# Third layer's attention: outputs scaled in place of probabilities, and TensorE visits it every second slot

## The reference, cut to what matters

```python
proj = y @ w_in; q, k, v = split(proj)                     # stage in3
s = einsum('bqhgd,bjhd->bhgqj', q_c, k_c) * scale + bias
p = softmax(where(valid, s, -inf))                         # p / sum(p)
o = einsum('bhgqj,bjhd->bqhgd', p, v_c)
return o.reshape(B, S, C_DIM) @ w_out                      # stage out3
```

## Time and profile before

| | us |
|---|---|
| runs | 2072.51, 2074.53, 2071.71 (median 2072.51) |
| profiled execution | 2075.14 |
| its span | 2073.3 |
| TensorE busy in it | 2055.2 |
| VectorE busy | 1180.8 |
| ScalarE busy | 759.5 |

### The profile page before, as it was taken

The page is one execution under the profiler, slowest core; times in us unless marked ns, Lnnn a source line. Parts: engine busy times, 40 slices in busy tenths (PEclk is TensorE's granted clock), DMA queues, the critical chain, the costliest instruction groups (busy, mean ns, idle before and its releaser), DMA issues.

```text
span 2073.3 us, 27109 instructions
## 1 busy us (share of the span) xinstructions
PE 2055.2 (99%) x10366; PEld 1689.7 (81%) x10366; DVE 1180.8 (57%) x1927; ACT 759.5 (37%) x1163; POOL 123.8 (6%) x138
## 2 busy tenths in 40 slices
PE   9999999999999999999999999999999999999999
PEld 7888888778888888988788888888876688888887
DVE  5444433786444433487778666633668877666433
ACT  5222222354322222463454322222557753222222
POOL 0000000400000000000002000000413120000001
PEclk9999999999999999999999999999999999999999
DMA  8322233312222222331221322233347622232222
GB/s 255 121 98 101 76 99 108 130 47 96 86 101 101 96 69 98 116 102 62 92 82 62 101 101 101 76 99 109 103 128 166 158 78 102 101 101 95 72 96 82
DMA packets 78300, 210.90 MB, mean 102 GB/s; under 512 B 46192, under 2 KB 49568, under 8 KB 61840
## 3 DMA queue, kind: packets, MB, share of 16 engines
q1 hardware_dynamic: 72896, 184.04, 28.0%
q0 software_dynamic: 2992, 12.31, 2.1%
q10 hardware_dynamic: 2336, 13.52, 1.8%
HBM read 195.08 MB, written 7.38 MB: 98 GB/s over the span
## 4 chain that ended last, share of the span: by engine, by line
PE 88%; DVE 6%; ACT 3%; issue 1%; DMA 1%; POOL 0%; SPq 0%; ACTq 0%; DVEq 0%
PE ps L1184 28%; PE ps L1185 28%; PE ps L1186 28%; ACT weigh L561 2%; DVE w_lo L1629 1%; PE ps L684 1%; DVE weigh L576 1%; DVE halves L583 1%; PE ps L666 1%; ACT w_hi L1621 1%; PE ps L651 1%; DVE weigh L593 1%; DMA h<-in_x_t 0%; ACT x_split L1707 0%; PE ps L1171 0%
## 5 line engine op out<-in xcount | busy, mean ns | idle before, releaser
L1184 PE MATMUL ps<-x_split,w_hi 128*128 128x512 f32 (+1 forms) x1774 | 697.6, 393 | 1.2 <-DVE x_split L1667 1.2
L1186 PE MATMUL ps<-x_split,w_lo 128*128 128x512 f32 (+1 forms) x1774 | 688.3, 388 | 0.0
L1185 PE MATMUL ps<-x_split,w_hi 128*128 128x512 f32 (+1 forms) x1774 | 688.1, 388 | 0.0
L1611 ACT ACTIVATE w_hi<-raw 128x2048 fp32r<-128x2048 f32 (+3 forms) x144 | 242.2, 1682 | 495.2 <-PE ps L1186 492.3
L1184 PEld LDWEIGHTS ps<-x_split,w_hi 128*128 128x128 f32 x1774 | 333.3, 188 | 79.2 <-issue 12.5
L1639 DVE TENSOR_TENSOR w_lo<-raw,w_hi 128x2048 fp32r<-128x2048 f32 (+3 forms) x144 | 287.9, 1999 | 179.7 <-ACT w_hi L1611 179.2
L1186 PEld LDWEIGHTS ps<-x_split,w_lo 128*128 128x128 f32 x1774 | 333.2, 188 | 68.5
L1185 PEld LDWEIGHTS ps<-x_split,w_hi 128*128 128x128 f32 x1774 | 333.5, 188 | 66.5 <-issue 1.0
L1184 PE MATMUL ps<-act,w_hi 128*128 128x512 f32 (+1 forms) x1026 | 376.9, 367 | 3.4 <-DVE w_lo L1629 3.1
L1185 PE MATMUL ps<-act,w_hi 128*128 128x512 f32 (+1 forms) x1026 | 372.9, 363 | 0.0
L1186 PE MATMUL ps<-act,w_lo 128*128 128x512 f32 (+1 forms) x1026 | 372.7, 363 | 0.0
(11 more groups left out here) (248 smaller groups left out, 1760.3 us busy)
## 6 DMA issues: line engine op xcount, KB each, us to landing
raw<-in_w_up SPq DMA_DIRECT2D x87, 1024.0 KB, 4.9
raw<-in_w_down SPq DMA_DIRECT2D x29, 768.0 KB, 4.2
raw<-in_w_in SPq DMA_DIRECT2D x20, 1024.0 KB, 4.9
raw<-in_w_down SPq DMA_DIRECT2D x29, 640.0 KB, 3.8
raw<-in_w_out SPq DMA_DIRECT2D x8, 1024.0 KB, 4.9
raw<-in_w_in ACTq DMA_DIRECT2D x8, 1024.0 KB, 5.5
skew<-scratch POOLq DMA_DIRECT2D x1, 5120.0 KB, 32.4
biases<-skew POOLq DMA_DIRECT2D x16, 256.0 KB, 4.3
```

Of the source, the lines that this page charges most:

```text
L1184: pe.matmul(own, hi, rhs_hi, start=start, stop=False)
L1185: pe.matmul(own, hi, rhs_lo, start=False, stop=False)
L1186: return pe.matmul(own, lo, rhs_hi, start=False, stop=stop)
L1611: eng.activation(w_hi[:, w], raw[:, w], ACT.Copy).then_inc(hi_rounded, 1)
```

## The change

- `SLOTS`: the first 22 slots lie at steps 88, 93, 98, 104, ... 200 (before: 21 slots at 84, 89, 94, ... 190), the last seven at 203, 206, 210, 213, 217, 220, 224 (before: eight at 196, 200, ... 224).
- TensorE does nothing in odd slots. In even slot i it does the scores of units i and i+1 and then the value products of units i-5 and i-4.
- VectorE no longer scales probabilities. It copies the halves first, then writes the reciprocals of the sums to `OUT_INV`. Eight times SP stores the reciprocals of a chunk to DRAM (128 partitions x 8 values of 4 bytes, the order turned) and loads them back as two rows, each broadcast over 64 partitions.
- When a chunk's value products are done and its factors have landed, VectorE multiplies the bank by the factors into `mix_raw` (new, slot 3c+7, for odd c below 7 slot 3c+8); ScalarE takes the high part from there, and VectorE the low part one slot later (for c = 7 in slot 28 too).
- The clearing of `ssum`, whose place holds factors, moves from the start of out3 to the end of its first pass.
- In in1 and in2 the transposes of the values move from 14 to 12 steps before the end.

```diff
-SLOTS = {84 + 16 * i // 3 if i < 21 else 196 + 4 * (i - 21): i for i in range(29)}
+SLOTS = {88 + 16 * i // 3 if i < 22 else 203 + 7 * (i - 22) // 2: i for i in range(29)}
+        MIX_AT = {NPARTS * c + 7 + (c % 2 if c < KD - 1 else 0): c for c in range(KD)}
+        REST_AT = {i + int(c < KD - 1): c for i, c in MIX_AT.items()}
 def slot_pe(pe, i):
+            if i % 2:
+                return
+            for u in (i, i + 1):
+                if u < STEPS:
+                    scores_pe(pe, u)
+            for u in (i - 5, i - 4):
+                if 0 <= u < STEPS:
+                    values_of_unit_pe(pe, u)
 # values_of_unit_pe: the bank of chunk c is free when
-                if s == 0 and c >= 2: pe.wait_ge(w_mix, c - 1)
+                if s == 0 and c >= 2: pe.wait_ge(w_mixed, c - 1)
+        def factors_out_sp(sp, c):
+            sp.wait_ge(w_inverted, NPARTS * (c + 1))
+            if c >= 2:
+                sp.wait_ge(w_mixed, c - 1)
+            rows = factors[c % 2 * 2:c % 2 * 2 + 2, :].rearrange("h (n q) -> q h n", q=P)
+            sp.dma_start(rows, inverses_of(c), allow_slow_non_contiguous=True).then_inc(f_written, 16)
+        def factors_in_sp(sp, c):
+            sp.wait_ge(f_written, 16 * (c + 1))
+            for hh in range(2):
+                row = factors[c % 2 * 2 + hh:c % 2 * 2 + hh + 1, :]
+                sp.dma_start(factor_rows[c % 2][64 * hh:64 * hh + 64, :], row.to_broadcast([64, T])).then_inc(f_landed[c % 2], 16)
 # SP, in its loop over units u (c, s = divmod(u, NPARTS)), after slot_sp(sp, u)
+                        if s == 0 and c:
+                            factors_in_sp(sp, c - 1)
+                        if s == NPARTS - 1:
+                            factors_out_sp(sp, c)
+                    factors_in_sp(sp, KD - 1)
 # slot_act: the high part
-                eng.wait_ge(w_weighed, NPARTS * (c + 1))
-                eng.activation(chunk(mix_hi, c), pair_bank(c), ACT.Copy).then_inc(w_mix_hi, 1)
+            if i in MIX_AT:
+                c = MIX_AT[i]
+                eng.wait_ge(w_mixed, c + 1)
+                eng.activation(chunk(mix_hi, c), chunk(mix_raw, c), ACT.Copy).then_inc(w_mix_hi, 1)
 # slot_dve
-                link(eng.reciprocal(INV[:, part_col(u, n=rows)], ROW[:, part_col(u, n=rows)]))
-                for part, (n, at_, n_keys) in enumerate(own):
-                    for hh in range(2):
-                        p = weigh_at(u, hh)[:, at_:at_ + n_keys]
-                        ins = eng.tensor_scalar(p, p, INV[:, part_col(u, part, hh)], None, ALU.mult)
                 eng.tensor_copy(to, words).then_inc(w_halved, 1)
+                if s == 0 and c >= 2:
+                    eng.wait_ge(f_written, 16 * (c - 1))
+                sums = ROW[:, part_col(u, n=rows)].rearrange("p (n h) -> p h n", h=2)
+                eng.reciprocal(inverses_of(c)[:, :, own[0][0]:own[0][0] + len(own)], sums).then_inc(w_inverted, 1)
+            if i in MIX_AT:
+                c = MIX_AT[i]
+                eng.wait_ge(w_weighed, NPARTS * (c + 1))
+                eng.wait_ge(f_landed[c % 2], 32 * (c // 2 + 1))
+                eng.tensor_tensor(chunk(mix_raw, c), pair_bank(c), factor_rows[c % 2], ALU.mult).then_inc(w_mixed, 1)
+            if i in REST_AT:
+                c = REST_AT[i]
                 eng.wait_ge(w_mix_hi, c + 1)
-                eng.tensor_tensor(chunk(mix_lo, c), pair_bank(c), chunk(mix_hi, c).bitcast(F32), ALU.subtract).then_inc(w_mix, 1)
+                eng.tensor_tensor(chunk(mix_lo, c), chunk(mix_raw, c), chunk(mix_hi, c).bitcast(F32), ALU.subtract).then_inc(w_mix, 1)
 # VectorE, out3: link(eng.memset(ssum[:, :], 0.0)) moves from before to behind the loop over the first pass
 # in1 and in2, TensorE and ScalarE
-                    if g == end - 14:
+                    if g == end - 12:
```

More of the change, by code:

```diff
@@ L166, in repeat, with build @@
         body(i)
-def build(nc, x_t, vecs, weights, mixer_consts, pool_tab, small_consts, pool_w, sinks, rel_bias, out_t, scratch, skew, stop=None):
+def build(nc, x_t, vecs, weights, mixer_consts, pool_tab, small_consts, pool_w, sinks, rel_bias, out_t, scratch, skew, factors, stop=None):
     names = [s.name for s in STAGES]
@@ L330, in build @@
         w_probs = sem("w_probs")
-        w_normed = sem("w_normed")
+        w_inverted = sem("w_inverted")
+        f_written = sem("f_written")
+        f_landed = [sem(f"f_landed{k}") for k in range(2)]
+        w_mixed = sem("w_mixed")
         w_halved = sem("w_halved")
@@ L487, in part_col @@
             return slice(4 * (u % 4) + 2 * part + hh, 4 * (u % 4) + 2 * part + hh + n)
-        def slot_pe(pe, i):
[L491 to L501, removed]
-                    for hh in range(2):
[L503 to L519, removed]
@@ new lines, in scores_pe @@
+        def scores_pe(pe, i):
+            c, s, own, _ = blocks_of(i)
+            if i == 0:
+                pe.wait_ge(w_v_done, KD)
+            if s == 0:
+                pe.wait_ge(evacuated, IN3.g0 + 2 * c + 2)
+            if i >= 2:
+                pe.wait_ge(w_max, rows_up_to(i - 1))
+            ks = (2 * c + 1) % 6 * T
+            for n, at_, w in own:
+                qs = 2 * c % 6 * T + n * P
+                for hh in range(2):
+                    rows = slice(64 * hh, 64 * hh + 64)
+                    ins = pe.matmul(score_bank(i, hh)[:, at_:at_ + w], ring[rows, qs:qs + P], ring[rows, ks:ks + w],
+                                    start=True, stop=True)
+            ins.then_inc(w_scores, 1)
@@ new lines, in values_of_unit_pe @@
+        def values_of_unit_pe(pe, u):
+            c, s, own, _ = blocks_of(u)
+            pe.wait_ge(w_copied, u + 1)
+            if s == 0 and c >= 2:
+                pe.wait_ge(w_mixed, c - 1)
+            for n, at_, w in own:
+                for j in range(n + 1):
+                    for hh in range(2):
+                        vc = (c // 4 * NB + j) * T + c % 4 * P + 64 * hh
+                        ins = pe.matmul(pair_bank(c)[64 * hh:64 * hh + 64, n * P:(n + 1) * P], v_tok[:, vc:vc + 64],
+                                        turned_at(u)[:, hh, at_ + j * P:at_ + (j + 1) * P], start=j == 0, stop=j == n)
+            ins.then_inc(w_weighed, 1)
@@ L528, in slot_sp, with inverses_of @@
                                    halves_at_slot(u, 4 * w)).then_inc(w_crossed[u % 2], 16)
+        def inverses_of(c):
+            return OUT_INV[:, c % 2 * 2 * NB:(c % 2 + 1) * 2 * NB].rearrange("p (h n) -> p h n", n=NB)
+        def factors_out_sp(sp, c):
[6 more added lines that the diff above has]
+            sp.wait_ge(f_written, 16 * (c + 1))
+            for hh in range(2):
+                row = factors[c % 2 * 2 + hh:c % 2 * 2 + hh + 1, :]
+                sp.dma_start(factor_rows[c % 2][64 * hh:64 * hh + 64, :], row.to_broadcast([64, T])).then_inc(f_landed[c % 2], 16)
         def pair_load_act(eng, step):
```

16 lines of the change are left out of this document (7 added, 9 removed).

## The result

| | before | after |
|---|---|---|
| median of 5 runs each, us | 2073.05 | 2106.22 (2103.46 to 2113.76) |
| ratio | | 1.0165 [1.0146, 1.0183] |
| profiled execution, its span | 2075.14, 2073.3 | 2103.46, 2101.6 |

The changed kernel is 33 us slower. The forecast was 2064.4 us, with a range to 2071.0.

A forecast was written before the change was run, and what follows sets the result against it. TensorE, busy 2055 of 2073 us, was taken as the bound; visits -7.0, ring -1.8, step 209 +0.3, end of first pass +2.1, value transposes -1.7 took 2072.5 to 2064.4 us, range 2058.5 to 2071.0.

The forecast's parts named there:

- The factors' DMAs: Storing and loading each chunk's factors: 4 us plus 3, hidden by four slots, 5 us of room at chunk 7; cost 0.
- a store that lands later than 9 us: Factor stores to DRAM: a landing this late was listed among the signs that the forecast is wrong.
- The rival on this side: Slow single-value stores: SP stands behind each, transposes and value products come late; 2082 at 30 us; chance 0.07.
- Visits: TensorE's visits to scores and values fall from 28 to 15, 14.7 us to 7.7: gain 7.0, at worst 4.6.
- seam: Rival: two units' scores in a row lose time between them, and layers 1 and 2 gain nothing: 2068.5; chance 0.13.
- Ring: TensorE's scores waiting for a ring tile: gain 1.8 us, bounds 1.9 and minus 6.
- Step 209, chunk 7: TensorE waits 2.4 us for step 209's rest, clock falls, 0.3 us more than before; then 1.0 us for chunk 7.
- The fifth tile: End of out3's first pass: the fifth tile's pair complete at 9.45 against 8.5, so 0.95 us late.
- Value transposes: Layers 1 and 2: transposing the values two steps later removes two waits; gain 1.7 us, bounds 0 and 1.9.
- Sum: All terms together: -7.0 - 1.8 + 0.3 + 2.1 - 1.7 = -8.1 us, from 2072.5 to 2064.4.
- the wait for `turned`: Value products waiting for ScalarE's `turned` copy: listed among the signs that the forecast is wrong.
- the end of the first pass: Unit 23's late values delay chunk 7, the next tile and the fifth: cost 2.1 us, bounds 0.5 and 3.5.

The follow-up runs named there:

- B: The changed kernel with each store of 1024 single values replaced by the same 4 KB as two whole rows of other data, waits and loads kept: 2066.43 us, 0.9967.
- D: The kernel before with new slots, paired visits, later value transposes, probabilities scaled as before, plus eight stores of 1024 single values nobody waits for: 2099.86 us, 1.0118.
- K: The changed kernel with two-row stores, and beside each a store of 1024 single values 64 bytes apart: 2070.23 us, 0.9981.
- G: The changed kernel with each factor store written as 128 pieces of 32 bytes in place of 1024 of 4: 2066.37 us, 0.9966.
- L: The changed kernel with two-row stores, and beside each a store of 128 single values 64 bytes apart: 2066.17 us, 0.9967.
- C: The kernel before with the new slots, paired visits and later value transposes, probabilities scaled as before, no factors: 2072.52 us, 0.9995.
- F: The changed kernel's output scaling with the visits and slots of the kernel before, without factor stores, loads and their waits: 2067.17 us, 0.997.
- O: The changed kernel without factor stores and loads, slot 23 of VectorE and ScalarE moved from step 206 to 209: 2063.17 us, 0.9951.
- J: The changed kernel with two-row stores, and beside each a store of 128 single values side by side, 4 bytes apart: 2096.24 us, 1.0098.
- A: The changed kernel without its eight stores of reciprocals and sixteen loads of factors: 2065.53 us, 0.9962.

## Why the prediction was wrong

**The step that failed** is "The factors' DMAs": "I take 4 for the store and 3 for the loads", and then "Cost 0; bounds 0 and, above 12 us for store and loads together, the excess". The store took 9.4 to 12.7 us. That is the prediction's own sign of being wrong, a store that lands later than 9 us. But the landing is the smaller part of the price. At chunk 7 store and loads took 13.5 us, which costs TensorE a wait of 5.5 us where B has 0.9; D shows 27 us with nobody waiting for any landing. The step priced a DMA by who waits for it, and put at nothing what it does to the other transfers in flight: for some 8 us behind the first store the DMAs moved 20 to 76 GB/s in place of 172 to 398 in B, and weight loads, bias tables and transposes all come late. The rival on this side had the chance 0.07, and its mechanism (SP standing, the last chunk late) and its price (2082) were those of the landing as well. The nearest row, the transpose, was no bound: it never writes single words to DRAM.

The page that I cited against the store, *DMA: Bandwidth & Descriptors* of the Trainium skill ("Rules for kernel authors"), is right on the count: from 1515 to 1700 us SP's and ScalarE's queue q1 has 51,472 packets after and 43,472 in B. But K has 51,792 and is only 4 us above B, so the count sets no price here. Nor does a piece below 512 B, the other rule cited there: G's pieces of 32 bytes and L's of 4 cost nothing.

**The other steps**, read in B, where only the grain of the store differs:

- *Visits.* No seam: two units' scores of 384 and 128 + 256 columns take 1.50 us to what follows, 6 x 0.213 + 0.22, and the values of two units 1.68:

```profile
1549.19 1.57 PE L512 MATMUL ps<-ring 64*128 64x128 f32 x12
1550.69 1.75 PE L526 MATMUL ps<-turned,v_tok 128*64 128x128 f32 x28
1552.37 0.50 PE L1229 MATMUL ps<-x_split,w_hi 128*128 128x512 f32 x1
1552.71 0.40 PE L1230 MATMUL ps<-x_split,w_hi 128*128 128x512 f32 x1
```

- *Ring.* No score waits for it. Without scaled outputs (C) scores wait 3.6 us in three, and the pairs alone gain next to nothing. That the relief is a condition for them is the likely reading, not a tested one.
- *Step 209, chunk 7.* Predicted 2.4 us and a fall of the clock, then 1.0; measured 2.3, 0.91 and 0.9. The fifth tile, predicted 0.95 late, waits 0.2. TensorE's waits and one window in B:

```profile
PE ps L1229 <- DVE w_lo L1674: 2.5, 2, 2.3
PE ps L1229 <- DVE x_split L2119: 1.0, 1, 1.0
PE ps L1229 <- DVE act L638: 0.9, 1, 0.9
PE ps L526 <- ACT turned L586: 0.4, 1, 0.4
```

```profile
1640.00:1660.00 20.00, 17.26 (x111) 12.99 (x111) 11.11 (x21) 12.22 (x18) 0.00 (x0) 0.91 0.66 146
```

- *Value transposes.* After, L1525 (L1485 before) has no wait for `proj` tiles of VectorE, where there were 1.7 us; alone it was not run.
- *Sum.* 2064.4 forecast, 2066.4 measured in B. Most of the 2.0 us between them is the base: the forecast started from 2072.5, and the kernel before took 2073.9 in B's series. B gains 7.5 us where 8.1 were forecast. The loads and their waits (0.9) and the wait for `turned` (0.4) had stood at nothing, and the end of the first pass came cheaper than its 2.1, so the closeness is in part luck.

Why 40 us: in the profiles of this attention TensorE waits 30.5 us after and 4.8 in B, 25.7 more, and the windows of the clock (13.6 us against 1.8) give 11.8; together 37.5, for spans 37.2 apart. What the chain below a late transfer does is seen; why one falls on `w_lo` and another on the reductions was not followed for each.

There is also a wrong part in what the terms were worth one by one. In F's expectation I took the rest at step 209 as late in the old layout too. F shows that scaled outputs alone take it away (no wait there at all), and the pairs bring it back with two slots ahead of it. So scaled outputs in the old visits gain 5.8 us, and the pairs 1.6 more, or 4.0 more once slot 23 is moved (O).

## What to carry to other kernels

Price a DMA twice: by who waits for it, and by what every other transfer in flight loses; many releasers late at once and low GB/s while transfers are due are the sign of the second. The DMA share is no sign: it was high behind one such store and zero behind another. Don't let a store put neighbouring words of DRAM from different partitions one by one: turn the tile on chip first, or write 32 bytes a piece, as here. And where two work items come in a row ahead of a deadline, move one behind it: the wait at step 209 went for one number in a table.

## What the runs showed of the hardware that was not expected

- 128 values of 4 bytes, stored beside a row store eight times: 30 us if side by side, 2.5 if 16 bytes apart, nothing if 64 apart; whole 32-byte pieces side by side nothing. 512 and 1024 single values cost 43 and 40, so the price hardly grows with the count. The last store of the changed kernel took 10 us, the last 6 of them with no packet of any transfer in the record.
- The cause behind that stays open. That several DMA engines contend for one piece of DRAM fits, and so does that small writes to one piece follow each other, whichever engine makes them; no row shows which engine writes which word.
- *VectorE: DVE Perf Modes* of the Trainium skill ("The three transpose paths") names a large innermost destination stride as what makes a plain copy with a transposing access pattern far slower than the DMA transpose. Here that stride doesn't set the price: one partition's values lie 512 bytes apart in the changed kernel (40 us) and 8192 bytes apart in K (4 us), and J has one value per partition (30 us).
- A wait of 2.3 us at the same place left the clock at 1.00 in A and brought the mean of the window to 0.91 in B. So in this case a wait of that length alone doesn't tell whether the clock falls.
